# Merging equal experts on two engines, the first-layer splits moved to VectorE, and the gate writes spread anew

## What is computed

```python
def peer_rows(xr, wq, k1, k2, u_tab, v_tab):
    ...
    v1, i1 = lax.top_k(s1, PEER_TOPK)
    v2, i2 = lax.top_k(s2, PEER_TOPK)
    cand = (v1[..., :, None] + v2[..., None, :]).reshape(L, PEER_HEADS, PEER_TOPK * PEER_TOPK)
    best, flat = lax.top_k(cand, PEER_TOPK)
    ...
    expert = row * N_KEYS + col
    gate = jax.nn.softmax(best, axis=-1)
    u_sel = jnp.take(u_tab, expert, axis=0)
    act = jax.nn.gelu(jnp.einsum('lhkd,ld->lhk', u_sel, xr).astype(f32), approximate=False)
    coef = (gate * act).astype(xr.dtype)
    return jnp.einsum('lhk,lhkd->ld', coef, jnp.take(v_tab, expert, axis=0))
```

## Time and profile before

| what | value |
|---|---|
| time, median of 3 runs | 4090.75 us (4078.49 to 4093.39) |
| the profiled execution: its time, its span | 4087.66 us, 4085.9 us |
| TensorE busy | 3421.8 us (84%), mean granted clock 0.911 |
| VectorE busy | 2347.9 us (57%) |
| ScalarE busy | 1613.9 us (39%) |
| GpSimd busy | 1592.9 us (39%) |
| moved by DMA | 777.68 MB, mean 190 GB/s |

### The profile page before, as it was taken

The page is one execution under the profiler, slowest core; times in us unless marked ns, Lnnn a source line. Parts: engine busy times, 40 slices in busy tenths (PEclk is TensorE's granted clock), DMA queues, the critical chain, the costliest instruction groups (busy, mean ns, idle before and its releaser), DMA issues. The chain is left out here.

```text
span 4085.9 us, 49425 instructions
## 1 busy us (share of the span) xinstructions
PE 3421.8 (84%) x16719; PEld 2942.9 (72%) x16719; DVE 2347.9 (57%) x4549; ACT 1613.9 (39%) x4554; POOL 1592.9 (39%) x1194
## 2 busy tenths in 40 slices
PE   5998798999898966767887667666659999999998
PEld 4997544447798966767887666666648888887887
DVE  3415443444588565564114454555448888898985
ACT  3322243433222576677882111111124444444443
POOL 1000200000000316556775777777757777421210
PEclk9999688889899988888998888888879999999999
DMA  2122391003111322222226666667679999999994
GB/s 78 46 84 101 132 405 38 1 5 115 51 40 49 104 67 66 67 64 82 82 86 248 235 249 252 242 255 253 238 273 390 389 386 371 366 394 394 400 350 162
DMA packets 258837, 777.68 MB, mean 190 GB/s; under 512 B 51872, under 2 KB 153376, under 8 KB 216128
## 3 DMA queue, kind: packets, MB, share of 16 engines
q1 hardware_dynamic: 186240, 415.74, 28.9%
q0 software_dynamic: 70656, 352.78, 22.6%
q10 hardware_dynamic: 1728, 6.49, 0.4%
HBM read 658.87 MB, written 115.56 MB: 190 GB/s over the span
## 5 line engine op out<-in xcount | busy, mean ns | idle before, releaser
L1506 POOL DMA_INDIRECT scratch_gates<-routes_merged,routes_at x768 | 963.8, 1255 | 275.3 <-issue 224.7
L1992 PE MATMUL val_acc<-n_hi 128*128 128x512 f32 x1536 | 599.7, 390 | 62.0 <-DVE n_lo L2027 61.0
L1993 PE MATMUL val_acc<-n_lo,n_hi 128*128 128x512 f32 x1536 | 599.0, 390 | 0.0
L1994 PE MATMUL val_acc<-n_hi,n_lo 128*128 128x512 f32 x1536 | 598.9, 390 | 0.0
L122 PE MATMUL route_hidden<-n_hi,route_u_hi 128*128 128x384 f32 x1152 | 412.3, 358 | 202.7 <-ACT route_hidden_out L1453 166.4
L1564 DVE CUSTOM_DVE_ANT_0 sparse_rows<-sparse_rows,mixed 128x1024 f32<-128x1024 f32 x288 | 351.6, 1221 | 375.0 <-DMA sparse_rows<-in_uv_rows,routes_at 340.4
L122 PE MATMUL hid_hidden<-n_hi,hid_u_hi 128*128 128x384 f32 x864 | 334.9, 388 | 251.7 <-DVE hid_u_lo L1457 251.7
L1553 POOL DMA_INDIRECT sparse_rows<-in_uv_rows,routes_at x256 | 357.6, 1397 | 458.8 <-DVE mixed L1587 388.6
L1964 ACT ACTIVATE n_hi<-val_v_raw 128x1024 fp32r<-128x1024 f32 x256 | 270.8, 1058 | 480.5 <-PE val_acc L1994 419.9
L123 PE MATMUL route_hidden<-n_lo,route_u_hi 128*128 128x384 f32 x1152 | 408.6, 355 | 0.0
L124 PE MATMUL route_hidden<-n_hi,route_u_lo 128*128 128x384 f32 x1152 | 407.2, 353 | 0.0
(11 more groups left out here) (289 smaller groups left out, 6689.3 us busy)
## 6 DMA issues: line engine op xcount, KB each, us to landing
val_v_raw<-in_v_rows SPq DMA_DIRECT2D x256, 512.0 KB, 6.8
scratch_gates<-zeros POOLq DMA_DIRECT2D x32, 1536.0 KB, 57.5
val_gate<-scratch_gates SPq DMA_DIRECT2D x256, 192.0 KB, 7.2
val_coef<-scratch_hidden SPq DMA_DIRECT2D x256, 192.0 KB, 7.6
route_u_raw<-in_peer_u SPq DMA_DIRECT2D x72, 512.0 KB, 3.7
scratch_hidden<-route_hidden_out SPq DMA_DIRECT2D x144, 192.0 KB, 1.9
hid_u_raw<-in_peer_u SPq DMA_DIRECT2D x54, 512.0 KB, 5.5
scratch_hidden<-hid_hidden_out SPq DMA_DIRECT2D x108, 192.0 KB
```

Of the source, the lines that this page charges most:

```text
L1506: pool.indirect_dma_start(self.t["gates"].rearrange("c r (l o) -> (c r l) o", o=1), bass.IndirectOffsetOnAxis(ap=self.routes.at[:, i, slot ...
L1992: nc.tensor.matmul(out, c_hi[:, s, tok], v_hi[:, s, to], start=(j == 0), stop=False)
L1993: nc.tensor.matmul(out, c_hi[:, s, tok], v_lo[:, s, to], start=False, stop=False)
L1994: last = nc.tensor.matmul(out, c_lo[:, s, tok], v_hi[:, s, to], start=False, stop=(j == KEYS - 1))
```

## The change

The merge: ScalarE still writes the 16 squares of part q, then one Relu(1 - 4 x square) over all 16 x 128 values, which is 1 where the experts are equal and 0 elsewhere. VectorE multiplies that by the gates and sums it (two instructions). The 16 Relus with accumulator go, and so does the wait of ScalarE for VectorE in the middle of a part.

The splits: `split_low` in routing moves from GpSimd to VectorE, and stands between the steps of the routing tiles. Where it stands is set by a running sum of planned costs, `spent`: one split for each 6.6 us planned (SPLIT_PERIOD), a merge part counted as 4.6. ScalarE does the squares and the Relu of part q behind the work of chunk `splits[0] - 2`, where `splits[0]` is the number of splits that VectorE has issued ahead of its multiply of part q. GpSimd has only scatters left in routing.

The spread: routing makes 78 chunks (was 72), the hidden stage 48 (was 54). Scatters: 330 in routing, 140 in the hidden stage, 298 in value pass one. Sparse units: 116 in the hidden stage, 72 in the 128 steps of value pass one, 100 in the first 108 steps of pass two.

```diff
-EARLY_RETRIEVE, EARLY_ROUTE = 2, 72
+EARLY_RETRIEVE, EARLY_ROUTE = 2, 78
...
-MERGE_FROM, BLEND_STEP = 9, 4
-SCATTER_FROM, SCATTER_STEP = 20, 4
-HIDDEN_SCATTERS = 560
-HIDDEN_UNITS = 140
+PAUSES, MERGE_LAG, MERGE_COST = 10, 4, 4.6
+SPLIT_PERIOD = 6.6
+SCATTER_FROM, ROUTE_SCATTERS = 17, 330
+HIDDEN_SCATTERS = 470
+HIDDEN_UNITS, FIRST_PASS_UNITS = 116, 72
...
-            def sums(act, q):
-                i, first = dense_at(q)
-                act.wait_ge(blended, q + 1)
-                for s in range(CHUNK_SLOTS):
-                    last = nc.scalar.activation(same[:, q % 2, s], same[:, q % 2, s], ACT.Relu,
-                                                accum_out=routes.merged[:, i, first + s:first + s + 1])
-                last.then_inc(routes.merged_ready, 1)
...
+                def merge(q):
+
+                    i, first = dense_at(q)
+                    dve.wait_ge(same_ready, q + 1)
+                    link(nc.vector.tensor_tensor(same[:, q % 2], same[:, q % 2],
+                                                 routes.gate[:, i].unsqueeze(1).to_broadcast([P, CHUNK_SLOTS, HK]), ALU.mult))
+                    nc.vector.tensor_reduce(routes.merged[:, i, first:first + CHUNK_SLOTS], same[:, q % 2], AX.X,
+                                            ALU.add).then_inc(routes.merged_ready, 1)
+
+                def split_due():
+                    while splits[0] < EARLY_ROUTE and spent[0] >= splits[0] * SPLIT_PERIOD:
+                        early.split_low(nc.vector, dve, splits[0])
+                        splits[0] += 1
+
+                def pause(cost):
+
+                    spent[0] += cost
+                    pauses[0] += 1
+                    q = len(same_at)
+                    split_due()
+                    if q < CHUNKS_OF * DENSE_TILES and pauses[0] >= PAUSES * (q // CHUNKS_OF + 1) + MERGE_LAG + q % CHUNKS_OF:
+                        same_at.append(max(0, splits[0] - 2))
+                        merge(q)
+                        spent[0] += MERGE_COST
+                        split_due()
...
+                    act.wait_ge(squared, q + 1)
+                    nc.scalar.activation(same[:, q % 2], same[:, q % 2], ACT.Relu, scale=-4.0, bias=1.0).then_inc(same_ready, 1)
...
-        used = spread_evenly(left, STEPS - 20) + [0] * 20
+        used = spread_evenly(FIRST_PASS_UNITS, KEYS) + spread_evenly(left - FIRST_PASS_UNITS, KEYS - 20) + [0] * 20
```

More of the change, by code:

```diff
@@ L1665, in _ @@
[L1665 to L1699, removed]
+            exp_at, same_at = [], []
             @block.vector
@@ L1702, in _ @@
             def _(dve):
-                steps = [0]
+                steps, spent, pauses, splits = [0], [0.0], [0], [0]
                 def link(instruction):
@@ L1742, in tile @@
                     link(last)
+                    pause(5.7)
                     for s in range(2):
@@ L1771, in _ @@
-                for q in range(blended_to, merged_end):
-                    blend(dve, q)
+                while len(same_at) < CHUNKS_OF * DENSE_TILES:
+                    pause(0.0)
+                while splits[0] < EARLY_ROUTE:
+                    pause(SPLIT_PERIOD)
+            @block.tensor
+            def _(pe):
+                for j in range(EARLY_ROUTE):
+                    for n in range(ND):
+                        early.multiply(pe, j, n)
+            @block.gpsimd
+            def _(pool):
+                for j in range(EARLY_ROUTE):
+                    scatter.issue(pool, route_scatters[j])
@@ new lines, in _, with pairs @@
+            @block.scalar
+            def _(act):
+                def pairs(q):
+                    i, first = dense_at(q)
+                    if first == 0:
+                        act.wait_ge(routes.routed, i + 1)
+                    if q >= 2:
+                        act.wait_ge(routes.merged_ready, q - 1)
+                    for s in range(CHUNK_SLOTS):
+                        last = nc.scalar.activation(same[:, q % 2, s], expert[:, i], ACT.Square, scale=-1.0,
+                                                    bias=expert[:, i, first + s:first + s + 1])
+                    last.then_inc(squared, 1)
+                    act.wait_ge(squared, q + 1)
+                    nc.scalar.activation(same[:, q % 2], same[:, q % 2], ACT.Relu, scale=-4.0, bias=1.0).then_inc(same_ready, 1)
+                early.split_high(act, 0)
+                early.split_high(act, 1)
+                for j in range(EARLY_ROUTE):
+                    for n in range(ND):
+                        early.activate(act, j, n)
+                    if j + 2 < EARLY_ROUTE:
+                        early.split_high(act, j + 2)
+                    for i in range(TILES):
+                        if exp_at[i] == j:
+                            m = tokens_of(ROUTE_ORDER[i])
+                            act.wait_ge(maxed, i + 1)
+                            nc.scalar.activation(shifted[:m], shifted[:m], ACT.Exp).then_inc(exp_done, 1)
+                    for q in range(CHUNKS_OF * DENSE_TILES):
+                        if same_at[q] == j:
+                            pairs(q)
```

36 lines of the change are left out of this document (13 added, 23 removed).

## The result

The changed kernel takes 4120.21 us (median of 7 runs, 4105.72 to 4131.34), the kernel before on the same chip 4095.39 us (7 runs, 4078.49 to 4099.51). The ratio is 1.0068, with a 95% interval of 1.0046 to 1.009. The profiled execution has a span of 4118.3 us; before it was 4085.9.

A forecast was written before the change was run, and what follows sets the result against it. Bounds were taken as ScalarE in routing, GpSimd in the hidden stage, TensorE in the value passes. 91 - 259 + 51 + 60 = -57 against the profiled 4087.7 gave 4031, as a median 4034 us; range 3930 to 4115.

The forecast's parts named there:

- routing to the first gather: Routing: VectorE's queue with its waits takes 949 us, so the hidden stage begins at 2258 instead of 2167, +91 us.
- hidden stage: Hidden stage: fewer GpSimd instructions, six gather buffers late next, 11.6 us a step, 564 us instead of 823, -259 us.
- value pass one: Value pass one: GpSimd becomes the bound with 298 scatters and 69 gathers, 575 us, +51 us.
- value pass two: Value pass two: DMA at 401 GB/s takes 4.71 us a step, +69; nearly that was taken, +60 us.
- the loop: Routing: ScalarE's part waits for an earlier chunk, VectorE's split stands behind the merge; VectorE waits 5.9 us 48 times, 283 us.
- Rival A: Routing: the loop does not bind, the stage takes 702 us, 247 less than 949, total 3790; chance 6%.
- two late gathers: Hidden stage: 57% of steps have two gathers startable only after an add of the same step; last dot ends at 12.7 us.
- GpSimd's scatters no longer end it: Sign for the hidden stage: its end is no longer set by GpSimd's scatters; steps of 11 to 12 us.
- At 401 GB/s 4.71 us: Value pass two: 1.89 MB a step at 401 GB/s takes 4.71 us, +69 us over 108 steps.
- Rival D: All stages: routing +115, hidden step 11.9 us, passes +65 and +75, total 4090, no change that can be told; chance 17%.
- rival B: Hidden stage: landing of gathers into six buffers keeps the step near 14.7 us, total 4176, slower; chance 13%.

The follow-up runs named there:

- one_chunk_earlier: The changed kernel with ScalarE's squares and Relu of a merge part placed one chunk further ahead (splits - 3, was splits - 2): 3888.17 us, 0.9504 of the kernel before.
- short_adds: The changed kernel with the adds of the last 100 sparse units, in value pass two, working on 64 of 1024 columns: 4122.15 us (one run).

## Why the prediction was wrong

All four mechanisms were there, each with its sign. What failed is the size of the terms: every one was off the same way, the hidden stage most. Measured by the marks in place of the forecast:

| term | forecast | measured | off |
|---|---|---|---|
| routing to the first gather | +91 | +110.8 | +20 |
| hidden stage | -259 | -227.8 | +31 |
| value pass one | +51 | +75 | +24 |
| value pass two | +60 | +75 | +15 |
| sum | -57 | +32.4 | +89 |

- **Routing.** The chain of the loop held. VectorE waited 324.6 us for Relus, where waits and lost clock were put at 283 + 36 = 319; its own work with the gaps between instructions was 625 us against 630. What the sum lacked is that VectorE also waits for ScalarE's rounded half before a split, 19.0 us, and that is nearly the whole miss. Rival A put the price of the loop at 247 us; one_chunk_earlier measured 238. That the waits come out so near is partly luck: the sum had 48 waits of 5.9 us, as if each part took the same, and the trace has 35 of 9.3 us, the longest 15.5.
- **Hidden stage.** "11.3 us, and I add 0.3 for a scatter in the way": it was 12.0. The share of steps with two late gathers was right (57% forecast, 24 of 44 counted), and so nearly was the step with one (9.5 forecast, 9.8 measured). The step with two was mis-sized, 12.7 forecast and 14.5 measured: the sum has the second gather start 3.4 us behind the first add and land 8.0 us later, and in the trace it starts after 3.6 and lands 9.8 us later (mean of 16), of which its issue alone is 3.05, where the earlier trace rows has a mean of 1.47. 48 steps make 19 us of the miss. The stage's end was set at 5 us behind the last chunks; TensorE's last matmul starts at 2860.5 and GpSimd's last scatter at 2870.9, so "GpSimd's scatters no longer end it" was wrong as well.
- **Pass one.** The price of a scatter, 1.58, was right (1.56). GpSimd's scatters ended 594 us after the stage's start, not 575, for it waited 21.7 us once, at 2905, for an add that frees a buffer. And from the first load of pass two to its first matmul it took 19.5 us, not 13.5: the multiply for pass two stands ahead of pass one's last split, so that TensorE still had a step of pass one to do when the load was there.
- **Pass two.** "At 401 GB/s 4.71 us": in the 400 us above it ran at 390, 4.92 a step, and over the 108 steps with units at 4.86. That is 17 us more. The sum also counted from 4.07 us a step, where the kernel before took 4.17 over the same 108 steps, which is 11 us the other way, and took 60 of its own +69. Together these give the +15. VectorE was not the bound, as short_adds shows; the rate taken was the highest of any row instead of a mean. The earlier trace rows had only 100 us, and the same kernel before makes 394 over 400 us. The Trainium skill, *DMA: Bandwidth & Descriptors*, section Bandwidth, has 425 GB/s for large transfers of a single core. The trace does not reach that in either value pass.

The decision for "faster" rested on a sum of four terms, a gain of 259 and losses of 202. Each measured term lies inside the ends that the prediction gave it, but its upper ends (+125, -181, +78, +85) add up to +107, 4198 us, and the stated range stopped at 4115, as if the errors would partly cancel. All four went the same way, by something left out each time (a second wait, a longer second gather and a tail, one wait and the order at a boundary, a rate that was the best and not the mean), and +20, +31, +24 and +15 are more than the whole forecast gain. Rival D, "all is given back", with a chance of 17%, came nearest in its terms: those for routing and the passes (+115, +65, +75) are within 10 us of those measured; its hidden step of 11.9 and the tail behind it were still short. But its total is a slip: by its own terms, with 46 steps of 11.9 (-245), it is 4101 us and not 4090. And it forecast "no change" within 0.5%, while the kernel is slower by 0.7%; for slower the prediction had only rival B, whose hidden step near 14.7 us was not what happened, and one percent. The measured 4120 lay outside the range of 3930 to 4115.

What remains open: why the issue of the second late gather takes 3 us.

## What to carry to other kernels

A wait in an in-order queue costs those who stand behind it, so where a merge waits for another engine, ask how many steps ahead its input is asked for: one chunk earlier was worth 238 us here, with not one instruction changed. Before moving work off an engine, count the buffers that its products sit in; once GpSimd was relieved, six gather buffers set the step, and freeing them one step sooner gave 111 us. And where a forecast is a small difference of large terms, one direction of error in all of them turns its sign, so the range must reach towards the sum of their ends.

## What the runs showed of the hardware

*The issue of an indirect DMA on GpSimd has no single price.* In 15 us of the changed kernel's pass one, GpSimd and then VectorE in order of time:

```profile
3199.70 0.97 POOL L1507 DMA_INDIRECT scratch_gates<-routes_merged,routes_at  x1 [0.30 <-issue]
...
3202.26 0.98 POOL L1507 DMA_INDIRECT scratch_gates<-routes_merged,routes_at  x1 [0.30 <-issue]
...
3206.51 1.36 POOL L1507 DMA_INDIRECT scratch_gates<-routes_merged,routes_at  x1 [0.31 <-issue]
...
3209.78 1.36 POOL L1554 DMA_INDIRECT sparse_rows<-in_uv_rows,routes_at  x1 [0.31 <-issue]
...
3202.52 1.23 DVE L1565 CUSTOM_DVE_ANT_0 sparse_rows<-sparse_rows,mixed 128x1024 f32<-128x1024 f32 x1 [3.51 <-DMA sparse_rows<-in_uv_rows,routes_at]
...
3205.75 1.28 DVE L1588 SCALAR_TENSOR_TENSOR mixed<-sparse_rows,sparse_coef,mixed 128x1024 f32<-128x1024 f32 x1
3206.94 0.55 DVE L2040 TENSOR_TENSOR val_coef<-val_coef,val_gate 128x384 f32<-128x384 f32 x1
...
3209.02 1.28 DVE L1588 SCALAR_TENSOR_TENSOR mixed<-sparse_rows,sparse_coef,mixed 128x1024 f32<-128x1024 f32 x1
```

Beside a wait or the dot (L1565) an issue takes 0.97 to 0.98 us, beside VectorE's instructions with two inputs in SBUF (L1588, L2040) 1.36. Over 2950 to 3470 us the scatters say the same: 58 with VectorE idle took 0.97 us on average, 21 beside a dot alone 0.98, and 191 that met an instruction with two inputs 1.37, between 0.97 and 2.04. While VectorE waited at the pass's end (3452 to 3486 us) a scatter took 0.97 again (the row at 3474.29). The Trainium skill, *SBUF — State Buffer*, section Who interferes with whom, says that a VectorE instruction with two SBUF inputs contends with a GpSimd instruction that reads SBUF; these rows agree in kind for an indirect DMA, whose indices lie there, and show a delay of 0.4 us on average. That the inputs are the cause was not tried apart.

*TensorE's clock follows its pauses.* In routing the same 3744 matmuls were busy for 722 us at a granted clock of 0.85 and, without the waits for splits, for 671 us at 0.97. The 51 us are the part of the loop's price that shows as slower matmuls.
